# One stream for an input projection of nine tiles, expert keys applied after the queries, constants on a second queue

## What is computed

```
proj = rms_norm(x) @ w_in               # 1024 -> 3328 = 512 q, 512 k, 512 v, 1792 RWKV columns
ps   = p + (p_prev - p) * mu            # p: the RWKV columns; p_prev: the row before, zero ahead of row 0
mixed = concat(diff_attend(rope(q), rope(k), v), rwkv_time_mix(ps))
h    = x + mixed @ w_out
# PEER, for the rows hn = rms_norm(h):
q    = (hn @ wq).reshape(T, 8 heads, 2, 128)
s    = einsum('thcd,hcnd->thcn', q, sub_keys)        # 8 x 2 x 128 scores
# two top-16, then 16 of 256 pairs: 16 experts for each row and head
out  = sum over 8 x 16 experts of gate * gelu(u[e] . hn) * v[e]
```

## Time and profile before

| | us |
|---|---|
| median of 3 runs | 4084.86 |
| fastest and slowest run | 4084.67, 4087.32 |
| span of the profiled execution | 4092.8 |
| first gather issued in it | 812.3 |

### The profile page before, as it was taken

The page is one execution under the profiler, slowest core; times in us unless marked ns, Lnnn a source line. Parts: engine busy times, 40 slices in busy tenths (PEclk is TensorE's granted clock), DMA queues, the critical chain, the costliest instruction groups (busy, mean ns, idle before and its releaser), DMA issues.

```text
span 4092.8 us, 54673 instructions
## 1 busy us (share of the span) xinstructions
PE 2860.4 (70%) x20366; PEld 1365.7 (33%) x20366; DVE 2602.7 (64%) x5836; ACT 1289.0 (31%) x3603; POOL 1334.5 (33%) x1163
## 2 busy tenths in 40 slices
PE   5688989966577666757676676768666748756564
PEld 2365454533224222422332243224222415421111
DVE  1234265288749856884897499658856676444954
ACT  1112111143432433342434234433433134422232
POOL 0000000044434433442444244334333355533453
PEclk8898999977787787778778777878787567777665
DMA  7356714599999999999999999999999799999998
GB/s 266 118 187 217 277 48 162 208 413 414 414 397 411 415 409 401 375 410 408 402 410 403 399 410 414 396 391 409 381 412 379 290 376 409 375 376 372 405 402 361
DMA packets 319391, 1445.27 MB, mean 353 GB/s; under 512 B 28228, under 2 KB 64196, under 8 KB 179478
## 3 DMA queue, kind: packets, MB, share of 16 engines
q0 software_dynamic: 161792, 1157.70, 69.9%
q1 hardware_dynamic: 157334, 284.08, 19.4%
HBM read 1386.83 MB, written 54.85 MB: 352 GB/s over the span
## 4 chain that ended last, share of the span: by engine, by line
PE 38%; DMA 33%; DVE 19%; issue 5%; ACT 2%; POOL 2%; SPq 1%; another core or an unknown queue 0%; DVEq 0%; ACTq 0%; POOLq 0%
DMA pe_buf<-in_experts,pe_idx 23%; PE ip_B L987 9%; DVE pe_buf L2220 6%; DMA op_wkr<-scratch_wk_rows 6%; PE pe_psO L1367 5%; PE pe_B L1317 5%; PE pe_psH L1349 3%; PE pe_B L1300 3%; PE pe_B L1022 1%; PE pe_B L1271 1%; POOL pe_buf L942 1%; PE pe_B L1169 1%; DVE pe_top L1990 1%; PE pe_B L1120 1%; DMA ip_w<-in_w_in 1%
## 5 line engine op out<-in xcount | busy, mean ns | idle before, releaser
L942 POOL DMA_INDIRECT pe_buf<-in_experts,pe_idx x1088 | 1261.7, 1160 | 2706.3 <-PE pe_psO L1367 1738.8
L2220 DVE CUSTOM_DVE_ANT_0 pe_buf<-pe_buf,pe_hnR 128x1024 f32<-128x1024 f32 x1088 | 1319.7, 1223 | 826.3 <-DMA pe_buf<-in_experts,pe_idx 752.3
L1367 PE MATMUL pe_psO<-pe_buf,pe_Z 128*32 128x256 f32 x8704 | 812.3, 475 | 492.6 <-ACT pe_Z L1654 430.3
L1367 PEld LDWEIGHTS pe_psO<-pe_buf,pe_Z 128*32 128x32 f32 x8704 | 221.3, 123 | 1117.4 <-ACT pe_Z L1654 768.1
L1648 ACT ACTIVATE pe_gelu<-pe_dot 128x1 f32<-128x1 f32 x1088 | 216.6, 199 | 1081.9 <-DVE pe_dot L2220 1006.6
L987 PE MATMUL ip_B<-ip_w,ip_xT 128*128 128x512 f32 (+1 forms) x1008 | 427.4, 575 | 20.9 <-DMA ip_w<-in_w_in 20.1
L1349 PE MATMUL pe_psH<-pe_hn,pe_pick 128*128 128x512 f32 x544 | 395.0, 816 | 62.8 <-ACT pe_hnR L1630 60.9
L1317 PE MATMUL pe_B<-op_wkr,pe_mix 128*128 128x512 f32 (+1 forms) x576 | 299.9, 669 | 121.0 <-DMA op_wkr<-scratch_wk_rows 121.0
L1654 ACT ACTIVATE pe_Z<-pe_gl,pe_gelu 128x8 f32<-128x8 f32 x1088 | 327.2, 301 | 49.2 <-PE pe_psO L1367 4.9
L987 PEld LDWEIGHTS ip_B<-ip_w,ip_xT 128*128 128x128 f32 x1008 | 190.5, 194 | 224.1 <-issue 215.4
L1317 PEld LDWEIGHTS pe_B<-op_wkr,pe_mix 128*128 128x128 f32 (+1 forms) x576 | 114.6, 208 | 278.8 <-issue 278.2
(11 more groups left out here) (319 smaller groups left out, 3647.6 us busy)
## 6 DMA issues: line engine op xcount, KB each, us to landing
op_wkr<-scratch_wk_rows SPq DMA_DIRECT2D x36, 2048.0 KB, 18.9
ip_w<-in_w_in SPq DMA_DIRECT2D x24, 2048.0 KB, 9.0
op_w<-in_w_out SPq DMA_DIRECT2D x18, 2048.0 KB
pe_buf<-in_experts,pe_idx POOLq DMA_INDIRECT x1088
ip_w<-in_peer_wq SPq DMA_DIRECT2D x4, 2048.0 KB, 9.4
scratch_wk_rows<-ip_wkc SPq DMA_DIRECT2D x16, 512.0 KB, 4.4
tm_p<-scratch_kept_rows SPq DMA_DIRECT2D x8, 896.0 KB
out_p_all<-ip_o SPq DMA_DIRECT2D x27, 256.0 KB, 5.9
```

Of the source, the lines that this page charges most:

```text
L942: pool.indirect_dma_start(buf[b][:], None, T["experts"], bass.IndirectOffsetOnAxis(ap=idx[:, t % 2, h * NJ + j:h * NJ + j + 1], axis=0)).t ...
L1367: last = nc.tensor.matmul(psO[32 * x:32 * x + 32, j // 4, :], Z[:, n % NZ, 24 - 8 * turn:56 - 8 * turn], buf[n % NBUF][:, D + x * QUART:D ...
L2220: nc.vector.tensor_tensor_reduce(buf[b][:, 0:D], buf[b][:, 0:D], hnR[:, n // PH % 2, :], 1.0, 0.0, ALU.mult, ALU.add, dot[:, n % (NBUF):n ...
```

## The change

- **One stream.** The projection is now one list `IP` of steps: all units in the order of passes (0), (1, 2, 3, 4), (5, 6, 7, 8), with half turns of x between them. A half turn is four transposes into the bank `psW` and one multiplication by DVE. Tiles 1 to 3 are turned among the units of tile 0, tile 4 after the first units of the second pass, 5 to 8 around the border of the second and third. There is one wait less at the start of a pass: a unit waits for its own tile's turn, for its bank and for its chunk. w_in is read three times. `FILL` cuts the list at `IP_FIRST` (step 22) and `IP_HALF` (step 78 of 147).
- **Keys unfolded.** `fold_keys`, `wk_rows` and their buffers are gone. `op` makes the queries, turned: for each of four chunks of 2 MB of peer_wq 4 x 8 matmuls of 128x128, a copy by ACT (`op_qT`), and four matmuls of 128x128 with the keys, of which SP loads four chunks of 256 KB for every tile. `op` has 40 steps (32 before) at a cost of 2.0 (2.2).
- **Later rows.** `load_p` of the next tile is issued at the end of `op` (step 39, after the last scores), not at step 25: the keys lie where `p` does.
- **Zero row.** `moved_rows` has a row of zeros ahead; every tile loads 128 rows.
- **Constants** and the store of `moved_shift` are issued by POOL, after the first unit.

```diff
-FILL = (((("ip", (0,)),),),
-        ((("ip", (1, 2)), ("wk", None), ("ip", (3, 4))), (("gap", 10), ("tm", 0), ("at", 0), ("op", 0))),
-        ((("ip", (5, 6, 7, 8)),), (("tm", 1), ("at", 1), ("op", 1)), (("topk", 0),)))
+PASSES = ((0,), (1, 2, 3, 4), (5, 6, 7, 8))
+UNITS = tuple((t, n) for tiles in PASSES for n in range(NG) for t in tiles)
+def turns_after(g):
+    t, n = UNITS[g]
+    if g < NG - 1:
+        return [(g // 2 + 1, g % 2)]
+    early = {(1, 0): [(4, 0)], (2, 0): [(4, 1)], (1, NG - 1): [(5, 0)], (2, NG - 1): [(5, 1), (6, 0)],
+             (3, NG - 1): [(6, 1)], (5, 0): [(7, 0), (7, 1)], (6, 0): [(8, 0), (8, 1)]}
+    return early.get((t, n), [])
+FILL = (((("ip", (0, IP_FIRST)),),),
+        ((("ip", (IP_FIRST, IP_HALF)),), (("gap", 4), ("tm", 0), ("at", 0), ("op", 0))),
+        ((("ip", (IP_HALF, IP_STEPS)),), (("tm", 1), ("at", 1), ("op", 1)), (("topk", 0),)))
 ...
-                    if t:
-                        sp.dma_start(ps[:], moved_rows[t * P - 1:t * P + P - 1, :]).then_inc(s["p_in"], 16)
-                    else:
-                        sp.dma_start(ps[1:P, :], moved_rows[0:P - 1, :]).then_inc(s["p_in"], 16)
+                    sp.dma_start(ps[:], moved_rows[t * P:t * P + P, :]).then_inc(s["p_in"], 16)
 ...
+            def constants():
+                pool.wait_ge(ip["done"], 1)
 ...
+                    if 19 <= k < 19 + 4 * NC:
+                        n_, j = (k - 19) // 4, (k - 19) % 4
 ...
+                        for n in range(KD):
+                            last = nc.tensor.matmul(B[:, n_ % 2, j * P:j * P + R], wqr[:, n_ % 2, n, j * P:(j + 1) * P],
+                                                    mix[:].rearrange("p (k t) -> p k t", k=KD)[:, n, 0:R],
+                                                    start=(n == 0), stop=(n == KD - 1))
+                    if k in (24, 28, 32, 36):
 ...
+                        for j in range(4):
+                            last = nc.tensor.matmul(B[0:R, 2 + n_ % 2, j * NK:(j + 1) * NK], op_qT[:, n_ % 2, j, 0:R],
+                                                    op_keys[:, n_ % 2, j, :], start=True, stop=True)
 ...
+                    if k in (23, 27):
+                        sp.wait_ge(op["q_done"], NC * t + (k - 19) // 4)
+                        load_wq((k - 23) // 4 + 2)
+                    if k in (26, 30):
+                        sp.wait_ge(op["scores_done"], NC * t + (k - 22) // 4)
+                        load_keys((k - 26) // 4 + 2)
+                    if k == OP_STEPS - 1 and t < LAST:
+                        load_after(t)
```

More of the change, by code:

```diff
@@ L242, in peer @@
     TOTAL = len(slots)
-    passes = [item[1] for streams in FILL for items in streams for item in items if item[0] == "ip"]
-    ip_units = [(t, n) for tiles in passes for n in range(NG) for t in tiles]
-    loads = [("w_in", n) for _ in passes[:WK_PASS] for n in range(NG)] + [("peer_wq", n) for n in range(NC)]
-    loads += [("w_in", n) for _ in passes[WK_PASS:] for n in range(NG)]
-    wk_first, wk_base = NG * WK_PASS, NG * sum(len(tiles) for tiles in passes[:WK_PASS])
-    wk_units = wk_order()
+    loads = [n for _ in PASSES for n in range(NG)]
     plan = pulls()
@@ L485, in peer @@
             op_hn = e.sb("hn", [P, D])
+        with ExitStack() as early:
+            e = Mem(nc, early, "op")
+            op_qT = e.sb("qT", [P, 2, 4, P])
+            e.sb("hold_h", [P, D])
+            op_keys = e.sb("keys", [P, 2, 4, NK])
         m.sb("small_part", [P, 4 * D])
@@ L548, in peer @@
             gate_ready""")
-        ip = sems("ip", "rope_in summed squared scaled turned xT done rotated copied split mu_in shift_in shifted shift_stored")
+        ip = sems("ip", "summed squared scaled turned xT done rotated copied split mu_in shift_in shifted shift_stored zero_in")
+        ip_rope_in = [m.sem(f"ip_rope_in{i}") for i in range(MOST)]
         ip_w_in = [m.sem(f"ip_w_in{i}") for i in range(2)]
@@ new lines, in project @@
+            def project(part):
+                for i in range(*part):
+                    kind, g, q_ = IP[i] if i < len(IP) else ("end", 0, 0)
+                    if kind == "turn":
+                        pe.wait_ge(ip_x_in[g % 2], 16 * (g // 2 + 1))
+                        if g or q_:
+                            pe.wait_ge(ip["xT"], 2 * g + q_)
+                        for k in range(4 * q_, 4 * q_ + 4):
+                            last = nc.tensor.transpose(psW[:, k % 4 * P:(k % 4 + 1) * P], ip_xs[g % 2][:, k * P:(k + 1) * P], ident[:])
+                        last.then_inc(ip["turned"], 1)
+                    if kind == "unit":
+                        t, n = UNITS[g]
+                        load = load_of(g)
+                        if q_ == 0:
+                            pe.wait_ge(ip["xT"], 2 * t + 2)
+                            if g >= 3 and UNITS[g - 3][1] < NQ:
+                                pe.wait_ge(ip["rotated"], rotated_of(g - 2))
+                            elif g >= 3:
+                                pe.wait_ge(ip["copied"], copied_of(g - 2))
+                            pe.wait_ge(ip_w_in[load % 2], 16 * (load // 2 + 1))
+                        for k in range(4 * q_, 4 * q_ + 4):
+                            last = nc.tensor.matmul(ipB[:, g % 3, 0:cols_of(n)], ip_xT[:, t % MOST, k, :],
+                                                    ip_w[:, load % 2, k, 0:cols_of(n)], start=(k == 0), stop=(k == KD - 1))
+                        if q_ == 1:
+                            last.then_inc(ip["done"], 1)
```

596 lines of the change are left out of this document (236 added, 360 removed).

## The result

The changed kernel takes 4057.9 us (4048.4 to 4066.2, 4 runs), the kernel before beside it 4086.1 us: a ratio of 0.9925 (95% interval 0.9899 to 0.9951). It is faster, by 28 us where 95 were forecast, and its time is above the range of 3955 to 4045 us. By spans the sum missed by 66 us (4064.4 against 3998), and 62 of them lie in one place, the gather stage.

A forecast was written before the change was run, and what follows sets the result against it. PE was taken as the bound to 811 us, DMA bytes in the gather stage. 4092.8 - 120 + 20 + 5 = 3998 us profiled; with the median 7.9 us below the span, 3990 us, 8-in-10 range 3955 to 4045.

The forecast's parts named there:

- Part 1: First tile, up to the second pass: starts at 80 us (72 to 95) instead of 135, 55 us gained.
- Part 2: Second and third pass: folding removed, first gather at 692 us against 812, 120 us sooner (77 to 145).
- The first rival: First 700 us: PE idle 70 us, not 32, by thinner filling and DVE at the third part's start; 4028 us, 15%.
- Part 3: Gather stage (3280 us): 20 us added for keys, PE's matmuls at nothing, 5 us for load places and later rows.
- the keys: Gather stage: tiles 2 to 8 each load 1.05 MB at 2.73 us a megabyte, unhidden, 20 us.
- The narrow matmuls: Gather stage: PE's 8 us more per tile lie in its idle third, at nothing.
- The third: Gather stage: PE's matmuls, place of the loads and later rows together cost 5 us, bounds -5 and 45.
- The premise behind it: Gather stage: DMA share 0.99 over 3280 us, so bytes bound it and every added megabyte costs its transfer time.
- The later rows: Tile heads in the gather stage: DVE's addition waits 0 to 8 us a tile for the later load.
- waits below 10 us: Sign in the trace afterwards: DVE's addition of the rows waits below 10 us for its load; above 24 us would be wrong.
- theory C: From the experiments: a byte in op's end goes into idle time, a byte at a tile's head costs its time.
- The gather stage gives half back: Rival: buffers run dry in every op, by third chunk then rows, 10 us for each of seven tiles; 4060 us, 12%.

The follow-up runs named there:

- the version without second product: Changed kernel with op's end in the kernel before's form (32 steps, 512-wide matmuls, early rows) and the product with the keys left out: 3964.1 us, ratio 0.9681.
- the eight copies: Kernel before, next tile's rows also copied into a scratch tensor: behind their load at op's step 25 4104.3 us, at op's last step 4127.9 us.

## Why the prediction was wrong

- **Part 1** held: 80 us forecast for the second pass (72 to 95), 84.5 found; no PE wait over 6.5 us ahead of it. The zero row does what was said: with 128 rows the engines move 243 to 425 GB/s in the 9 us behind 95.1. By the Trainium skill's rule on how many engines one DMA uses (DMA: Bandwidth & Descriptors, cited in the prediction) it had to, and the trace agrees. The first 80 us ran at 292 GB/s, near the 285 in the sum. The Trainium skill (Trainium Kernel Development and Optimization, Key Constraints) also says that issuing from another queue only saves issue time. That is what is seen: SP's next chunks go at 23.2 and 30.6 us while POOL issues the constants, and PE's waits for chunks stay near 20 us in sum, as before. What the prediction did not part are the two causes: the zero row and POOL's constants alone leave an 18.8 us wait for x.
- **Part 2** held: first gather forecast at 692, found at 696.7. The thin filling cost little: PE is idle for 35 us from 80 to 697 us, where 32 were in the sum. The first rival (the order doesn't fill) did not come.
- **Part 3 failed.** Of its three terms, the keys had 20 us and measured 0, twice. The narrow matmuls had 0 and measured 0. The third, "I take 5 us for all of this together; bounds -5 and 45", is the step that was wrong. The place of the loads and the later rows measured 29 us (the rows) and 22 us (reload and packing of the matmuls). To these come 21 us for the weight of `op` in the plan, which had no term at all (21 us with the rows early; 10 us, not clear of noise, in the changed kernel itself). Taken back one after the other, the three lead from 0.9925 to 0.9748, 72 us, and to 3988 us where 3990 had been forecast. The agreement is partly luck, since the keys' 20 us were not there.
- **The premise behind it** was read from one average: a share of 0.99 over 3280 us, "nothing hides them, since the engines are full". In shorter windows the same trace has 52 us at `op`'s end in which POOL issues 9 gathers, where it issues 17 in the 36 us of a tile's head. There chunks and rows keep the engines full: SP's queue has 41.8% of them in the 52 us, 11.2% on average. The Trainium skill (Perfetto Trace Analysis, Identifying the Most-Contended Engine) advises the rate over the engines' busy share for DMA. The trace agrees: 0.99 against 0.98 says little, 395 against 387 GB/s says 2%.
- **The later rows** were weighed by DVE's wait for them alone, 0 to 8 us a tile; that wait came out at 6.1 us in all, none of it in the gather stage. The test that I named for it, waits below 10 us, was met, and the load cost 29 us all the same, by its place; its bytes explain a part of that (theory C), the rest is open.
- **The plan's weight.** I followed `op`'s own steps from 2.2/247 to 2.0/256 of the window (this comes to 0.7 slots, not 0.6) and did not ask what the steps of time mixing do when `op` weighs 80 and not 70.4. In the earlier trace rows DVE at 39.1 of 45 us had shown how near its limit it is in that part of time mixing.
- **The rivals.** "The gather stage gives half back", 12%, had the time (4060) and the two places, the third chunk and then the rows: two edits there gave 22 and 29 us back. It did not have the waits. PE's wait for chunks fell, from 121.0 to 68.8 us over the gather stage (the waits of L1317 and L1261; waits for keys add 15.7), and DVE's for rows was nothing there.
- **Open:** 27 us between 0.9748 and 0.9681, the version without second product, of which 19 lie ahead of the first gather (704.5 against 685.6 in the profiled runs); which wait leaves the engines idle with late rows; why 40 steps cost 36 us more than 32; and what the reload and the packing of the matmuls gave each.

## What to carry to other kernels

Engines that are full on average can have one place in each period where a megabyte costs 1.2 us and another where it costs 2.9, as here. Look for both in short windows (16 gathers, some 40 us, here) before pricing a load, and price moving a load, not only adding one. When a stretch grows and its DMA rate stands, look at the stretch behind it. Where a table of costs sets the order, a change to one stage's weight moves all others: look for the stretch in which another engine is near its limit, and try the old total weight first. When a change wins in one stage and loses in another, take back its parts in the losing stage alone; here that made 0.75% into 2.5%.

## What the runs showed of the hardware

Adding or taking away 7.3 MB that SP's queue loads beside the gathers changed no time (0.9925 and 0.9923; 0.9853 and 0.9854), while 1.84 MB a tile, 14.7 in all, cost 17 us at one place and 43 us at the other, that is 1.2 and 2.9 us a megabyte against the 2.73 us that the queue's packets take by the earlier trace rows. Two of the eight copies fall before the first gather, which comes 4 and 10 us later by them (816.4 and 821.9). For the six behind it, 11.0 MB, this leaves 13 and 33 us, an estimate of 1.2 and 3.0 us a megabyte.

And the price of these float32 matmuls goes with their work, not with their number. These are the profile page's groups for the chunk matmuls over nine tiles, in the kernel before and the changed one (two records a matmul):

```profile
L1317 PE MATMUL pe_B<-op_wkr,pe_mix 128*128 128x512 f32 (+1 forms) x576 | 299.9, 669 | 121.0 <-DMA op_wkr<-scratch_wk_rows 121.0
```

```profile
L1261 PE MATMUL pe_B<-pe_mix,op_wq 128*128 128x128 f32 (+1 forms) x2304 | 317.0, 296 | 107.6 <-DMA op_wq<-in_peer_wq 68.8
```

Four times as many records take 6% more of PE, and the exchange alone cost no time (0.9687 against 0.9681).
